# Norms of a two-layer trunk: factor and addend joined with the next modulation's, the weight split placed behind the second tile, and the end by halves of the channels

## The reference

```
x <- LN0(ALPHA*x + 0.5*gate0*FFN1(mod0(x)))
x <- LN1(ALPHA*x + gate1*W_out[A|B|C|D](mod1(x)))
x <- LN2(ALPHA*x + 0.5*gate2*FFN2(mod2(x)))
mod_s(x) = x*(1 + scale_s) + shift_s      (scale and shift by token group, from c and w_mod)
LN(x)    = (x - mean)*rsqrt(var + EPS)*g + b
```

## Time and profile before

| what | value |
|---|---|
| median of 3 runs | 3151.21 us (3150.0 to 3159.24) |
| the profiled execution's own time | 3151.5 us |
| its span, first to last instruction | 3149.7 us |
| PE busy | 2954.1 us (94%) |
| VectorE busy | 1289.6 us (41%) |
| ScalarE busy | 904.8 us (29%) |
| ScalarE's split of a weight tile (w_split, 128x2048) | 1909 ns, x152 |
| mean granted TensorE clock | 0.967 |

### The profile page before, as it was taken

How to read it: one execution, slowest core, us unless ns; L and a number is a source line. 1 busy time by engine, 2 the same in 40 slices (tenths; PEclk the granted TensorE clock), 3 DMA queues, 4 the chain that set the end, 5 groups by cost and what they waited for, 6 DMA issues and landing times.

```text
span 3149.7 us, 46403 instructions
## 1 busy us (share of the span) xinstructions
PE 2954.1 (94%) x20109; PEld 2609.3 (83%) x20109; DVE 1289.6 (41%) x1813; ACT 904.8 (29%) x1262; POOL 35.2 (1%) x32
## 2 busy tenths in 40 slices
PE   6999999998899899999979999999988998999997
PEld 5999998776646599999979999977764556999996
DVE  3233226346555532322542332374283636223226
ACT  3221223323344322212251212233233524221222
POOL 0000000100000000000000000001000000000000
PEclk8999999999989999999989999999998999999998
DMA  9223233103220322322532232421132012223221
GB/s 302 67 60 95 67 122 118 54 27 108 71 70 14 94 74 61 87 80 78 159 105 76 65 92 64 145 73 54 54 108 85 30 27 94 67 68 86 76 60 52
DMA packets 359017, 259.03 MB, mean 82 GB/s; under 512 B 27152, under 2 KB 310100, under 8 KB 358740
## 3 DMA queue, kind: packets, MB, share of 16 engines
q1 hardware_dynamic: 358868, 256.85, 27.1%
HBM read 253.25 MB, written 3.57 MB: 82 GB/s over the span
## 4 chain that ended last, share of the span: by engine, by line
PE 87%; DVE 7%; ACT 2%; DMA 1%; SPq 1%; issue 1%; DVEq 0%; ACTq 0%; PEldq 0%
PE banks L738 56%; PE banks L653 16%; PE banks L603 2%; PE banks L1175 1%; PE banks L852 1%; PE banks L1198 1%; ACT arena L1261 1%; DVE x_res L1823 1%; PE banks L1212 1%; PE banks L1024 1%; PE banks L1168 1%; DVE w_split L1703 1%; PE banks L918 1%; PE banks L903 1%; PE banks L1118 1%
## 5 line engine op out<-in xcount | busy, mean ns | idle before, releaser
L738 PE MATMUL banks<-h_hi,w_split 128*128 128x320 f32 x5376 | 1185.1, 309 | 2.1 <-DVE mod L1652 2.1
L738 PEld LDWEIGHTS banks<-h_hi,w_split 128*128 128x128 f32 x5376 | 899.2, 188 | 2.9 <-issue 2.9
L738 PE MATMUL banks<-h_lo,w_split 128*128 128x320 f32 x2688 | 830.6, 309 | 0.0
L738 PE MATMUL banks<-hid_hi,w_split 128*128 128x320 f32 x2816 | 624.0, 309 | 0.1
L1261 ACT ACTIVATE arena<-banks 128x640 f32<-128x640 f32 (+8 forms) x336 | 170.7, 537 | 1235.8 <-PE banks L738 886.6
L1703 DVE TENSOR_TENSOR w_split<-w_slots,w_split 128x2048 fp32r<-128x2048 f32 x152 | 348.4, 2292 | 419.9 <-ACT w_split L1261 419.9
L738 PEld LDWEIGHTS banks<-h_lo,w_split 128*128 128x128 f32 x2688 | 504.6, 188 | 0.0
L738 PEld LDWEIGHTS banks<-hid_hi,w_split 128*128 128x128 f32 x2816 | 471.5, 188 | 1.7 <-issue 1.2
L738 PE MATMUL banks<-hid_lo,w_split 128*128 128x320 f32 x1408 | 435.1, 309 | 0.0
L1261 ACT ACTIVATE w_split<-w_slots 128x2048 fp32r<-128x2048 f32 x152 | 290.2, 1909 | 402.2 <-PE banks L738 397.0
L1767 DVE TENSOR_TENSOR arena<-arena,banks 128x640 f32<-128x640 f32 x88 | 72.2, 821 | 752.5 <-ACT arena L1261 752.5
(11 more groups left out here) (259 smaller groups left out, 2405.6 us busy)
## 6 DMA issues: line engine op xcount, KB each, us to landing
w_slots<-in_ffn_w_gu SPq DMA_DIRECT2D x176, 512.0 KB, 5.1
arena<-in_w_mod SPq DMA_DIRECT2D x14, 2048.0 KB, 12.7
w_slots<-in_ffn_w_down SPq DMA_DIRECT2D x64, 384.0 KB, 3.5
w_slots<-in_ffn_w_down SPq DMA_DIRECT2D x64, 320.0 KB, 4.2
h_mod<-in_w_mod SPq DMA_DIRECT2D x8, 2048.0 KB, 8.0
w_slots<-in_w_mod SPq DMA_DIRECT2D x8, 2048.0 KB, 7.9
mixed<-in_w_mod SPq DMA_DIRECT2D x6, 2048.0 KB, 9.2
w_slots<-in_w_in SPq DMA_DIRECT2D x6, 2048.0 KB, 7.8
```

The costliest lines, as they stand in the source:

```text
L738: ins = mm(banks[:, b0 + hf, 0:HALF], w[:, k, :], x[:, k, t], start=w is wlo and k == 0, stop=w is whi and x is hi and k == kt - 1, skip_g ...
```

## The change

The product with g and the addition of b leave the norms. VectorE makes, from g, b and the next modulation's rows, one factor and one addend for each channel and token group (`compose`, three instructions of 128x8 for each half of the channels, into `JOINT`), and `modulate` takes these and the tile that has only been multiplied by 1/std. `scale_residual` now applies ALPHA*g and ALPHA*b (`LNS`, made once) in eight instructions of 128x640 instead of one of 128x5120. The split of the next weights goes from before the second `shift` to behind the second tile. In sub-layer 2 of layer 0 ScalarE's loop over the tiles is gone, and `input_lo_tile` goes into VectorE's loop as in sub-layer 1. In layer 1's last norm nothing is joined. The mixers' ring brings pieces 12 and 14 (first halves of mod 2) where it brought 13 and 15, and norm 1 brings 13 and 15. At the end the ten groups go by halves of the channels: five token tiles of the first half, for which four tiles of X are enough, then five of the second; and SP stores after each copy (256 KB a DMA).

Left out here: renamed list entries, the semaphore counts, and where the moved pieces land.

```diff
@@ -148,7 +148,7 @@
-FIRST_MODS, RING_MODS, RING_AT = (0, 2, 1, 3, 4, 5), (10, 11, 13, 15), {1: 10, 3: 11, 5: 13, 7: 15}
+FIRST_MODS, RING_MODS, RING_AT = (0, 2, 1, 3, 4, 5), (10, 11, 12, 14), {1: 10, 3: 11, 5: 12, 7: 14}
 GATE_MODS = {0: (4, 5), 2: (16, 17)}
@@ -162,7 +162,7 @@
     if sub < 2:
-        return [((l, 8), (l, 9)), ((l, 12), (l, 14))][sub]
+        return [((l, 8), (l, 9)), ((l, 13), (l, 15))][sub]
     return [(l + 1, 2), (l + 1, 3)] if l + 1 < DEPTH else []
@@ -219,6 +219,8 @@
         MODS = [sb(f"mod_{l}", 144)[:].rearrange("p (s w m g) -> p s w m g", s=3, w=3, m=8) for l in range(DEPTH)]
+        LNS = [sb(f"ln_scaled_{l}", 48) for l in range(DEPTH)]
+        JOINT = sb("norm_mod", 32)[:].rearrange("p (w m g) -> p w m g", w=2, g=2)
         LB, LBN, OML = sb("lb", 4), sb("lb_next", 4), sb("one_minus_lb", 4)
@@ -495,7 +497,7 @@
                             else:
-                                sp.wait_ge(mod_row, mod_at[l, 14] + 1)
+                                sp.wait_ge(mod_row, mod_at[l, 15] + 1)
                             for i in GATE_MODS[sub]:
@@ -552,7 +554,7 @@
                 sp.wait_ge(s["side_done"], o["side_done"] + len(SIDE))
-                fill_mod(l, 12)
+                fill_mod(l, 13)
                 for d in range(2):
@@ -563,7 +565,7 @@
                 sp.wait_ge(s["new_ready"], o["new_ready"] + 1)
-                fill_mod(l, 14)
+                fill_mod(l, 15)
                 sp.dma_start(a["out_ckv"][0, l], NEWROWS[:, 0:P]).then_inc(s["small_store"], 16)
@@ -578,11 +580,13 @@
-            for t in range(NCH):
-                sp.wait_ge(fin_copy, 2 * t + 2)
-                dst = a["y_s"][0, t * P:(t + 1) * P, :] if t < 4 else a["y_p"][0]
-                sp.dma_start(dst, XIN[:, t, :]).then_inc(fin_store, 16)
-            sp.wait_ge(fin_store, 16 * NCH)
+            for n in range(2 * NCH):
+                half, t = n // NCH, n % NCH
+                cols = slice(half * 512, (half + 1) * 512)
+                sp.wait_ge(fin_copy, n + 1)
+                dst = a["y_s"][0, t * P:(t + 1) * P, cols] if t < 4 else a["y_p"][0, :, cols]
+                sp.dma_start(dst, XIN[:, t, cols]).then_inc(fin_store, 16)
+            sp.wait_ge(fin_store, 32 * NCH)
@@ -762,7 +766,7 @@
                             if l or sub:
-                                pe.wait_ge(mod_done, mod_at[l, 3 if sub == 0 else 14] + 1)
+                                pe.wait_ge(mod_done, mod_at[l, 3 if sub == 0 else 15] + 1)
                             for c in range(2):
@@ -1230,9 +1234,9 @@
-            pe.wait_ge(s["affine"], DEPTH * 24)
             for n in range(2 * NCH):
-                t, half = n // 2, n % 2
+                half, t = n // NCH, n % NCH
+                pe.wait_ge(s["affine"], 4 * half + 4)
                 if n >= 4:
@@ -1305,21 +1309,24 @@
-                    MOD = MODS[l]
+                    plain = l == 0 and sub == 0
+                    shift, scale = (MODS[l][:, sub, i] if plain else JOINT[:, i] for i in range(2))
                     for m in range(KT_M):
-                        if m % 4 == 0:
-                            act.wait_ge(mod_done, max(mod_at[l, 6 * sub + m // 4], mod_at[l, 6 * sub + 2 + m // 4]) + 1)
+                        if m % 4 == 0 and plain:
+                            act.wait_ge(mod_done, max(mod_at[l, m // 4], mod_at[l, 2 + m // 4]) + 1)
+                        elif m % 4 == 0:
+                            act.wait_ge(s["composed"], o["composed"] + 2 * (sub - 1) + m // 4 + 1)
                         if m == 0 and (l or sub):
-                            act.wait_ge(mod_row, mod_at[l, (3, 9, 14)[sub]] + 1)
+                            act.wait_ge(mod_row, mod_at[l, (3, 9, 15)[sub]] + 1)
                         if l or sub:
-                            act.wait_ge(s["affine"], o["affine"] + 8 * (sub - 1) + m + 1)
+                            act.wait_ge(s["normed"], o["normed"] + 8 * (sub - 1) + m + 1)
                         at = 8 * (sub // 2) + m
                             ins = f(dst[:, t0:t0 + n], X[:, m, t0:t0 + n], ACT.Identity,
-                                    scale=MOD[:, sub, 1, m, g:g + 1], bias=MOD[:, sub, 0, m, g:g + 1])
+                                    scale=scale[:, m, g:g + 1], bias=shift[:, m, g:g + 1])
                         ins.then_inc(s["modded"], 1)
@@ -1627,8 +1634,8 @@
                 layer_norm(2, (lambda: weights_hi(2 * FFN_JOBS + 1)) if l + 1 < DEPTH else None)
-                for m in range(KT_M):
-                    act.wait_ge(s["normed"], o["normed"] + m + 1)
+                for m in range(KT_M if l + 1 == DEPTH else 0):
+                    act.wait_ge(s["normed"], o["normed"] + 16 + m + 1)
                     f(X[:, m, :], X[:, m, :], ACT.Identity, scale=PTS1[l][:, R_LNG + 16 + m:R_LNG + 17 + m],
@@ -1663,6 +1670,7 @@
                     link(ins)
+                link(v.tensor_scalar(LNS[l][:], PTS1[l][:, R_LNG:R_LNG + 48], float(ALPHA), None, ALU.mult))
             dve.sem_inc(par1_ready, 1)
@@ -1702,13 +1710,31 @@
-                def input_lo_tile(sub, m):
-                    dve.wait_ge(s["h_hi"], o["h_hi"] + 8 * (sub // 2) + m + 1)
+                def input_lo_tile(n, m):
+
+                    dve.wait_ge(s["h_hi"], o["h_hi"] + 8 * n + m + 1)
                     v.tensor_tensor(HLO[:, m], GATE[:, m % 2], HHI[:, m].bitcast(F32), ALU.subtract).then_inc(s["h_lo"], 1)
                     dve.wait_ge(s["modded"], o["modded"] + 8 * (sub + 1))
-                    link(v.tensor_scalar(X, X, float(ALPHA), None, ALU.mult))
+                    if l == 0 and sub == 0:
+                        link(v.tensor_scalar(X, X, float(ALPHA), None, ALU.mult))
+                        return
+                    ln, at = (LNS[l], 8 * (sub - 1)) if sub else (LNS[l - 1], 16)
+                    for m in range(KT_M):
+                        ins = v.tensor_scalar(X[:, m, :], X[:, m, :], ln[:, at + m:at + m + 1], ln[:, 24 + at + m:25 + at + m], ALU.mult, ALU.add)
+                    link(ins)
+
+                def compose(sub, half):
+
+                    ln, sn = (l, sub + 1) if sub < 2 else (l + 1, 0)
+                    ms = slice(4 * half, 4 * half + 4)
+                    shift, scale = MODS[ln][:, sn, 0, ms], MODS[ln][:, sn, 1, ms]
+                    dve.wait_ge(mod_done, max(mod_at[ln, 6 * sn + half], mod_at[ln, 6 * sn + 2 + half]) + 1)
+                    gain, bias = (bc(PTS1[l][:, r + 8 * sub + 4 * half:r + 8 * sub + 4 * half + 4].unsqueeze(2), [P, 4, 2]) for r in (R_LNG, R_LNB))
+                    link(v.tensor_tensor(JOINT[:, 0, ms], scale, bias, ALU.mult))
+                    v.tensor_tensor(JOINT[:, 1, ms], scale, gain, ALU.mult)
+                    finish(v.tensor_tensor(JOINT[:, 0, ms], JOINT[:, 0, ms], shift, ALU.add), "composed", 2 * sub + half + 1)
@@ -1831,39 +1857,36 @@
                         mod_add(*mods[0], 3)
-                    if meanwhile:
-                        meanwhile()
+                        compose(sub, 0)
                     shift(1)
                     for m in range(KT_M):
+                        if m == 1 and mods:
+                            mod_add(*mods[1], 3)
+                            compose(sub, 1)
                         if m == 4 and meanwhile:
                             shift(3)
-                        if m == 1 and mods:
-                            mod_add(*mods[1], 3)
-                        if sub == 2:
-                            v.tensor_tensor(X[:, m, :], X[:, m, :], RS[:], ALU.mult).then_inc(s["normed"], 1)
-                            continue
-                        link(v.tensor_tensor(X[:, m, :], X[:, m, :], RS[:], ALU.mult))
-                        v.tensor_scalar(X[:, m, :], X[:, m, :], PTS1[l][:, R_LNG + 8 * sub + m:R_LNG + 8 * sub + m + 1],
-                                        PTS1[l][:, R_LNB + 8 * sub + m:R_LNB + 8 * sub + m + 1], ALU.mult, ALU.add).then_inc(s["affine"], 1)
-                        if sub == 1:
-                            if m >= 2:
-                                input_lo_tile(2, m - 2)
+                        v.tensor_tensor(X[:, m, :], X[:, m, :], RS[:], ALU.mult).then_inc(s["normed"], 1)
+                        if m == 1 and meanwhile:
+                            meanwhile()
+                        if m >= 2 and sub and mods:
+                            input_lo_tile(sub, m - 2)
                     if sub == 1:
                         weights_lo(FFN_JOBS + 1)
-                        input_lo_tile(2, 6)
-                        input_lo_tile(2, 7)
+                    if sub and mods:
+                        input_lo_tile(sub, 6)
+                        input_lo_tile(sub, 7)
                     weights_lo(0)
-                for m in range(KT_M):
-                    input_lo_tile(0, m)
-                    if l == 0 and m == 3:
-                        weights_lo(1)
+                    for m in range(KT_M):
+                        input_lo_tile(0, m)
```

(9 more changed lines are left out.)

1 line of the change is left out of this document (removed).

## The result

The changed kernel takes 3137.0 us, median of 6 runs (3135.16 to 3141.44), beside 3154.2 for the kernel before in the same comparison (6 runs, 3150.0 to 3159.24): a ratio of 0.9945, 95% interval 0.9935 to 0.9955. Measured again later beside other variants it was 3142.4 (6 runs), 0.9954 (0.9936 to 0.9971). The medians put the change at 13 to 17 us; 3135.5 was forecast, from a sum of 15.8.

What follows compares the result with a forecast made beforehand. PE bounds the kernel (87% of the chain), so only its waits can shrink. 2 x 0.0 + 2 x 2.3 + 8.2 + 3.0 = 15.8 off 3151.5 gives 3135.7, stated as 3135.5; range 3132 to 3139, with rivals 1 and 2 3131 to 3142.

Steps and rivals of the forecast that it cites:

- Norm 0: Before the mixers, twice: two added `compose` cost 0.60, dropped g, b and hand-over pay; gain 0.0 each.
- Norm 1: Before an FFN, twice: tiles 0.65 shorter on VectorE, PE starts 0.2 to 0.3 later; gain 2.3 us each.
- Norm 2: Layer 0: first remainder made earlier, PE starts 7.7 earlier; gain 8.2 us, bounds 7.0 and 9.5.
- The end: After the last norm: copies end 2.0 to 2.8 earlier, smaller last store; gain 3.0 us, bounds 1.8 and 3.6.
- The 0.65 for a last store of half the size: At the end: last DMA carries 256 KB instead of 512, at 406 GB/s 0.65 us less.
- the queue takes back up to 0.3: At the end: ten transfers need 6.5 us and start only at 3137.6, returning up to 0.3 us of the gain.
- rival 1: At the end: copies wait for VectorE, DMA rate bounds the stores, nothing gained; 3138.7 us, chance 0.05.
- Rival 2: VectorE's string is longer: small instructions take 0.5 (3140.1 us) or unwaited instructions don't overlap (3139.6); chance 0.08.
- Rival 3: Norms 1 and 2: VectorE and ScalarE only alternate, 3.0 us a tile; 3156.4 us, chance 0.09.
- Rival 4: Three tile-fed FFN products: granted clock stays at 1.2 GHz over all eight tiles; 3160.8 us, chance 0.04.
- the moved split's 0.25 us: Norm 1: 0.25 us at the start, subtracted from 3.25 along with 0.75 of ScalarE.

Runs made afterwards that it cites:

- the added waits: Changed kernel with a wait behind each of VectorE's eight products of a tile with 1/std, in every norm: 3148.5 us (one run).
- the reordered kernel: Changed kernel, first split before the second shift, ScalarE's second split ahead of norm 1's modulations, VectorE's behind the last remainder: 3133.2 us, 0.9926.

## Why the prediction was right, and where its terms were off

The time lies 1.5 us from the forecast and inside the range, and the mechanism at the norms came out as written; at the end two terms did not, and the sum there is right by luck. That the time comes so close is luck in part, too: the execution that was subtracted from is some 3 us faster than the median of before, and the medians' difference is 1.4 us larger than the sum.

- *Norm 0: right.* 8.38 and 8.34. The joined instructions were priced at 0.60 more, and the second `shift` comes 3.00 behind the first where it came 2.40 (532.11 to 535.11, and 532.69 to 535.09). Dropping g and b, and the hand-over, paid for them.
- *Norm 1: right, mis-sized by 0.2.* 2.49 against 2.3. PE starts 0.21 later (0.2 to 0.3 forecast). The seventh remainder came 0.3 earlier than the sum had it, since the sixth waited for ScalarE less long (0.44 where the sum has 0.8).
- *Norm 2: right.* PE 7.69 earlier (7.7), the product 8.00 (8.2). The slow stretch of PE was 4.9 us, between the 3.7 and 5.7 for which the sum was worked out both ways. Behind its first matmul PE waits for no remainder any more in this norm, so the stage is now PE's start, its work and that stretch.
- *The end: the sum right, two terms wrong.* By the copies 3.11 was gained (2.0 to 2.8 forecast): PE was at full clock by the fifth group and ten copies took 6.07, so 0.61 each and not 0.63. The 0.65 for a last store of half the size did not come at all, because the queue was still full of the nine before it. The prediction had this as "the queue takes back up to 0.3" and as rival 1; the tail is 2.62 MB at 382 GB/s, 6.9 us, and not 6.5. The two errors cancelled. Nor is 3.0 what every execution gets: against the changed kernel's second profile it is 2.0 (25.94 to 23.90), for the reason in the last section, and the trace of before has that packet among its stores as well.
- *Rival 1* (the end gains nothing) is refuted by 22.90 to 23.99 against 25.94 and 26.07, though its reason, the DMA rate, is what bounds the end now. *Rival 2* fell by the 0.16 us of the small instructions and by the 0.12 of a wait that the added waits showed. *Rival 3*, lock step: in norm 1 ScalarE waits for a remainder at two of its eight tiles, the third (1.23 us) and the fifth (0.66), not at each. The argument against it read too much out of the earlier trace rows: in the kernel before, too, ScalarE waited once, 1.69 at the fifth tile. *Rival 4*: the clock rose 3.3 us behind PE's start in norm 1 and 4.9 in norm 2 and stayed up through waits of 0.9.
- *The spread was too narrow upwards.* The profiled execution against which the sum was made, 3151.5, lies 3 to 4 us below the medians of before (3154.2, 3155.4, 3155.2, 3155.0), which three runs had not shown. Read as a difference, -15.8 lies between -17.2 and -12.7; read as a time, the second comparison's 3142.4 is just outside the range.

What the prediction did not see is that one part of the change works against the rest: it counted the moved split's 0.25 us at PE's start as a small debit of norm 1, and did not ask what the same kernel would be with the split left where it was. That is 0.6 at each norm 1 and 0.9 at norm 2.

Open is what sets the clock in the mixers. No experiment changed them, and the grants differ between executions of one kernel. Nor was the exchange of the modulation's pieces, or the longer `scale_residual`, tried by itself: the prediction has both at nothing, and what lies outside the mixers and the stages of the table took 1930.5 us before and 1930.6 after (1929 to 1931 over the other profiles), so nothing shows up there.

## What to carry to other kernels

Cost a change at the stage, from a landmark of the trace to the next one, and compare stages: here they repeat to 0.03 to 1.0 us, while whole executions of one kernel differ by 6 to 20. When work is moved out of one engine's way, see what was hiding it: the 2.2 us split delays the first tile by 1.2 where it stands in a wait (6.60 behind the first `shift` against 5.42), and everything behind it by its whole length where it doesn't. For a tail of stores look for the last one that finds the queue empty and count bytes from there; a smaller last store or an earlier first one gives nothing if the queue is full, or runs dry, in between.

## What the runs showed of the hardware

- The granted clock of a stage with many short gaps differs from execution to execution: by 4 us of 550 between two profiles of one kernel (547.5 and 551.5, mean clock 0.94 and 0.93), and in layer 0 by up to 13 over the twelve profiles (546.2 to 559.1), at the same 2874 matmuls. The Trainium skill, "TensorE: Matmul & The Clock Gate", section "What you observe", has half a microsecond of spread, either way, for one rise of the clock. The 496.6 and 502.8 us of PE above are more than that; that they are many such spreads added up is a reading, and not shown.
- An instruction packet among the stores lengthens the end by 1.0 us. Beside the stores the DMA engines also carry the instructions of the program, 16 KB at a time on one of the 16 engines, and such a packet took 0.96 to 1.16 us here. In the second profile of the changed kernel one falls at 3137.49, among the stores: the transfers pause at 3139, at their end one engine alone is still moving for 1 us (0.5 in the first profile), and the end stage is 1.0 us longer (23.90 against 22.90) with the copies at the same distances. The kernel with the split in front (23.99) and the one with the remainders behind the loop (23.83) have the packet among their stores as well; the first profile of the changed kernel, the new end alone and the reordered kernel (22.90 to 22.94) and the kernel with the added waits do not. That is three of three and none of four. No experiment moved the packet, so it is a correlation, with the late engine in the trace behind it. First the pause (windows), then what the queues carried from the first store to the end, second profile and first:

```profile
3138.00:3139.00 1.00, 0.00 (x0) 0.00 (x0) 0.79 (x2) 0.00 (x0) 0.00 (x0) 1.00 0.97 365
3139.00:3140.00 1.00, 0.00 (x0) 0.00 (x0) 0.00 (x0) 0.00 (x0) 0.00 (x0) 0.95 0.68 254
3140.00:3141.00 1.00, 0.00 (x0) 0.00 (x0) 0.00 (x0) 0.00 (x0) 0.00 (x0) 0.50 1.02 391
```

```profile
q1 hardware_dynamic: 1440, 2.62, 63.1%
q8 instruction: 1, 0.02, 0.7%
q14 instruction: 1, 0.01, 0.2%
```

```profile
q1 hardware_dynamic: 1440, 2.62, 74.6%
q14 instruction: 1, 0.01, 0.2%
```
